# Stick-breaking attention in a fused decoder layer: loads spread over groups, and score products of 64 rows in two halves of the array

## The chip, the cores and the metric

The kernel runs on one core of a Trainium2 chip. The metric is the device time of one execution in microseconds (us), as the median of three runs.

## What is computed

One layer of a hybrid decoder, for one sequence of 2048 positions (and 16 learned ones ahead of them), width 1024, all in float32. An input projection makes the streams of two branches: a recurrent one (RWKV-7, 16 heads) and an attention one (16 heads of 64). The attention is of the stick-breaking kind, without a softmax:

```
scale = SB_HEAD_DIM ** -0.5
logits = einsum("bhqd,bhkd->bhqk", q[qs:qe], k[:qe]) * scale
log_keep = where(visible, log_sigmoid(-logits), 0)        # visible: key before query
log_between = cumsum(log_keep, reverse=True) - log_keep
weights = where(visible, exp(log_sigmoid(logits) + log_between), 0)
out = einsum("bhqk,bhkd->bhqd", weights, v[:qe])
```

Both branches are gated, projected, merged and projected again, normalised and added to the input.

## The kernel before

The kernel has four stages in order. Two calls of `project_phase` (half A, then half B of the positions) make the streams and leave them in DRAM. `attention_phase` does the attention of all heads. Then come the recurrence's chunk loop and the output products.

**Projections.** A product over 1024 is made of three fp32r products (high and low parts of both sides). For the attention's queries and keys, ScalarE writes the high part out of PSUM, and VectorE subtracts it from the PSUM value to get the low part (`query_lows`, L716; `key_lows`, L708). SyncE stores four tensors, `q_hi`, `q_lo`, `k_hi` and `k_lo` (L256 to L270). TensorE waits for both parts before it uses a PSUM bank again (L450).

**Attention.** A head has 16 tiles of 128 queries; four tiles are a *group* of a *rank* 0 to 3. Rank 0 sees few keys and rank 3 all of them. `rank` (L886) orders the eight groups of two heads as 0 1 2 3 3 2 1 0. The texts below call these eight groups T0 to T7; T0 to T3 belong to the even head and T4 to T7 to the odd one.

For each query tile the keys are cut into pieces of at most 512 (`pieces_of`, L872), from the last keys to the first. A piece passes through the engines in this way:
- TensorE makes the scores `z` (L1104, L1105). The 128 rows of `q_parts` hold the queries' high part (64 rows) and low part (64 rows); `k_high` and `k_low` hold the key's part twice, once for each half of the rows. Two fp32r products thus add up all four combinations.
- ScalarE takes the sigmoid of the negated scores into `keep` (L1172).
- VectorE runs a product scan along the keys, from the last key to the first, into `kept` (L1207 for a tile's first piece, L1210 for the others). A scan starts from the last column of the piece before.

For each tile of 128 keys of a group (`turn`, L1107), TensorE transposes `kept` of up to four query tiles into `turned` (L1115), ScalarE copies it to `w` (L1182), and TensorE multiplies by *value steps* (differences of neighbouring values) into `acc` (L1142). The value products come in pairs of key tiles, each product in its own half of the array's columns. Three key tiles of lag separate transposes and value products. On the diagonal another table of steps, `dv_diag`, is used, whose last row is another row of DRAM, `v_edge`. The group's sum is made on VectorE (L1216) and multiplied by a gate (L1220), which gives y.

There are two PSUM banks for `z`, four for `turned`, four buffers for `keep` and eight for `w`. Queries, keys and value steps have two buffers each, one for the even and one for the odd head.

The order on TensorE, ScalarE and VectorE is written out by `attention_schedule` (L907): the logits of the next group are dealt out between the key tiles of this one (`merged`, L893). All engines follow this order.

**SyncE's queue** does all loads and stores of the stage, in order (L1058 to L1073). After the y of each group it stores y and loads the gate of the group after next. The loads of a whole head (`load`, L1028) are nine DMAs and come in one piece: that of the odd head after T0, that of the next even head after T3. Within one, the value steps (L1046), the diagonal's 127 rows (L1047) and the edge row (L1048) come last. TensorE waits for a head's six query and key DMAs before the first logits (L1086), and for all its v DMAs before the first value product (L1093).

```python
sp.dma_start(dv[u][:, first + 1:last + 1, :], by_tile[:, tiles, :]).then_inc(v_sem, 16)
sp.dma_start(dv_diag[u][0:P - 1, tiles, :], by_tile[0:P - 1, tiles, :]).then_inc(v_sem, 16)
sp.dma_start(dv_diag[u][P - 1:P, tiles, :], edge[:, tiles, :]).then_inc(v_sem, 16)
```

Of the kernel before, what the change touches and what calls it, by code (L numbers as in the profile page):

```python
# [60 lines left out]
def project_phase(nc, sem, t, io, scratch, half):  # L61
# [14 lines left out]
    BY_PART = [i for i in range(NG) if OWNER[i] in (BQ, BKS)]  # L76
    NP = len(BY_PART)
# [5 lines left out]
    with ExitStack() as ctx:  # L83
# [16 lines left out]
        dv, q_lo = sb("dv", [P, N]), [sb(f"q_lo{g}", [P, 512], F32R) for g in range(len(RG))]  # L100
        k_hi, k_lo, v_raw = raw[1][:, 1:].bitcast(F32R), raw[2][:, 1:].bitcast(F32R), raw[0]
# [23 lines left out]
        bg_sent, kh_sent, kl_sent = s_("bg_sent"), s_("kh_sent"), s_("kl_sent")  # L125
        parted, dv_done, ql_sent, edge_sent = s_("parted"), s_("dv"), s_("ql_sent"), s_("edge_sent")
# [8 lines left out]
        square_high, square_low = q_lo  # L135
# [37 lines left out]
        def parted_by(eng, k, i):  # L173
            eng.wait_ge(parted, NP * k + BY_PART.index(i) + 1)

# [4 lines left out]
        def _(sp):  # L180
# [26 lines left out]
            sp.sem_inc(kh_sent, 16 * G)  # L207
            sp.sem_inc(kl_sent, 16 * G)
            sp.sem_inc(ql_sent, 16 * len(RG))
# [36 lines left out]
            with sp.Fori(0, PAIRS) as k:  # L246
                for j in range(BLOCKS):
# [7 lines left out]
                    if j == BKS:  # L255
                        store_staged(k, BQ, "q_hi", 0)  # L256
                        for g, (at, size) in enumerate(RG):
                            parted_by(sp, k, AT[BQ] + g)
                            sp.sem_inc(sp_go, 1)
                            c = T0 + at - CHUNK  # L260
                            sp.dma_start(scratch["q_lo"][rows(k), c:c + size], q_lo[g][:, 0:size].bitcast(F32)).then_inc(ql_sent, 16)
                    if j == BVS:
                        for g, (at, size) in enumerate(SG):
                            c = slice(T0 + at, T0 + at + size)
                            evacuated(sp, k, AT[BKS] + g)
                            sp.sem_inc(sp_go, 1)
                            sp.dma_start(scratch["k_hi"][rows(k), c], k_hi[:, at:at + size].bitcast(F32)).then_inc(kh_sent, 16)
                            parted_by(sp, k, AT[BKS] + g)
                            sp.sem_inc(sp_go, 1)
                            sp.dma_start(scratch["k_lo"][rows(k), c], k_lo[:, at:at + size].bitcast(F32)).then_inc(kl_sent, 16)  # L270
# [53 lines left out]
            sp.wait_ge(kh_sent, 16 * G * (PAIRS + 1))  # L324
            sp.wait_ge(kl_sent, 16 * G * (PAIRS + 1))
            sp.wait_ge(ql_sent, 16 * len(RG) * (PAIRS + 1))
# [7 lines left out]
        def _(pe):  # L334
# [107 lines left out]
            with pe.Fori(0, PAIRS) as k:  # L442
                for j in range(BLOCKS):
                    b = (j + 1) % 2
                    pe.wait_ge(low, BLOCKS * k + j + 2)
                    for g, (at, size) in enumerate(FIRST[j]):
# [3 lines left out]
                        if OWNER[before] in (BQ, BKS):  # L450
                            parted_by(pe, earlier, before)
                        elif OWNER[before] >= BQ:
# [21 lines left out]
        def _(act):  # L474
# [12 lines left out]
            def raw_copy(k, b, g, at, size):  # L487
# [6 lines left out]
                if g == 0 and b == BK:  # L494
                    sent_all(act, kh_sent, k, G)
                if g == 0 and b == BV:
                    sent_all(act, kl_sent, k, G)
# [18 lines left out]
            def squares(k, g, at, size):  # L516
# [3 lines left out]
                if g:  # L520
                    now(act, norm_pe, k, g - 1)
                else:
                    sent_all(act, ql_sent, k, len(RG))
# [7 lines left out]
            def to_stage(k, j, g, size, func):  # L531
# [5 lines left out]
                act.activation(dst.bitcast(F32R) if j == BQ else dst, bank[slot(i)][:, 0:size], func).then_inc(staged, 1)  # L537
# [57 lines left out]
            with act.Fori(0, PAIRS) as k:  # L595
# [15 lines left out]
                for g, (at, size) in enumerate(SG):  # L611
                    i = AT[BKS] + g
                    made(act, k, i)
                    act.copy(k_hi[:, at + lead(at):at + size], bank[slot(i)][:, lead(at):size]).then_inc(staged, 1)
# [25 lines left out]
        def _(dve):  # L640
# [75 lines left out]
            def query_lows(k, g, at, size):  # L716
                i = AT[BQ] + g
                evacuated(dve, k, i)
                now(dve, norm_pe, k, G - 1)
                sent_all(dve, ql_sent, k, len(RG))  # L720
                dve.tensor_tensor(q_lo[g][:, 0:size], bank[slot(i)][:, 0:size], stage[store_of(i)][:, 0:size],
                                  ALU.subtract).then_inc(parted, 1)

# [63 lines left out]
            with dve.Fori(0, PAIRS) as k:  # L787
                dve.tensor_copy(cols[:, :], t["par"][:, bass.ds(N_COLS * k, N_COLS)]).then_inc(cols_done, 1)
                dve.wait_ge(cols_done, k + 1)
                for j in range(BLOCKS):  # L790
# [5 lines left out]
                    for g, (at, size) in enumerate(SG):  # L796
# [10 lines left out]
                        if j == BQ and g < len(RG):  # L807
                            query_lows(k, g, *RG[g])
                        if j == BKS:
                            operands(k, g, at, size)  # L810
                            bonuses(k, g, at, size)
                            key_lows(k, g, at, size)
# [94 lines left out]
def attention_schedule():  # L907
# [46 lines left out]
def attention_phase(nc, sem, t, io, scratch):  # L954
# [7 lines left out]
    last_logits = {e[1]: e[5] for e in order if e[0] == "logits"}  # L962
    last_values = {e[1]: e[3] for e in order if e[0] == "values"}
    with ExitStack() as ctx:
        sb = lambda name, shape, dt=F32: ctx.enter_context(nc.sbuf_tensor(name, shape, dt))
        ps = lambda name, shape: ctx.enter_context(nc.psum_tensor(name, shape, F32))
        q_parts = [sb(f"q_parts{b}", [P, SEQ], F32R) for b in range(2)]
        k_high = [sb(f"k_high{b}", [P, META + SEQ], F32R) for b in range(2)]
# [1265 lines left out]
```

## Time and profile before

| | |
|---|---|
| median of three runs | 4381.3 us (4378.88 to 4382.68) |
| the profiled execution, its own time | 4379.16 us |
| its span, from first to last instruction | 4377.4 us |
| TensorE (PE) products busy | 4171.0 us, 95% |
| VectorE (DVE) busy | 2380.5 us, 54% |
| ScalarE (ACT) busy | 1666.2 us, 38% |
| GpSimd (POOL) busy | 804.4 us, 18% |
| mean granted clock of TensorE | 0.977 |

How to read it: busy time is the time in which an engine had an instruction running. Products on TensorE overlap, so that a product's own duration (0.39 us) is longer than the distance from one to the next (0.23 us); distances between starts tell its pace. PEld is the loading of weights, which runs beside the products. SPq is SyncE's queue: a DMA instruction's duration there is the time for which the queue was held by it, not the transfer's. "[0.24 <-x]" behind a row is the idle time of the engine ahead of it and what ended it. PEclk is the granted clock of TensorE as a share of full speed.

### The profile page before, as it was taken

What the parts mean: (1) busy time and instruction counts of PE and PEld (TensorE: products, weight loads), DVE (VectorE), ACT (ScalarE), POOL (GpSimd) and SP (SyncE); (2) the same over time, 40 slices, a digit from 0 to 9 for tenths busy, and PEclk for the clock granted to TensorE, in tenths of its full rate; (3) what the DMA queues carried; (4) which work ended last, traced back from release to release, by engine and by line L of the source; (5) the groups of instructions that cost most, each with busy time, mean ns of one, the idle gap of its engine ahead of it and who ended that gap; (6) DMA issues with size and microseconds to landing.
All of it is one profiled execution on the core that took longest, in us unless ns stands there. A gap on an engine that the chain in (4) does not pass through costs nothing. (4 is left out here: it accounts for less than half of the span.)

```text
span 4377.4 us, 90822 instructions
## 1 busy us (share of the span) xinstructions
PE 4171.0 (95%) x35784; PEld 3344.7 (76%) x35784; DVE 2380.5 (54%) x3103; ACT 1666.2 (38%) x3296; POOL 804.4 (18%) x637
## 2 busy tenths in 40 slices
PE   7999999997999999997999999999899999999999
PEld 7888888985888888885555555655688888878887
DVE  5444444443444444442777777777467766743222
ACT  4222222223222222222666666666444444421111
POOL 2110111111111111110000000000256666610222
PEclk9999999998999999998999999999899999999999
DMA  2333433333333333334443442442233333355653
GB/s 93 109 117 119 122 109 110 102 115 110 109 118 116 109 104 118 107 103 113 89 94 69 82 93 63 87 94 62 75 114 99 101 104 100 92 184 177 189 188 129
DMA packets 486971, 479.74 MB, mean 110 GB/s; under 512 B 260610, under 2 KB 370818, under 8 KB 480914
## 3 DMA queue, kind: packets, MB, share of 16 engines
q1 hardware_dynamic: 475154, 450.33, 37.1%
q10 hardware_dynamic: 11520, 25.17, 1.6%
q8 instruction: 221, 3.62, 0.3%
q14 instruction: 76, 0.62, 0.1%
HBM read 305.45 MB, written 169.93 MB: 109 GB/s over the span
## 5 line engine op out<-in xcount | busy, mean ns | idle before, releaser
L1210 DVE TENSOR_TENSOR_SCAN kept<-keep,kept 128x512 f32<-128x512 f32 (+1 forms) x448 | 436.6, 975 | 63.1 <-ACT keep L1172 22.6
L1172 ACT ACTIVATE keep<-z 128x512 f32<-128x512 f32 (+3 forms) x704 | 343.4, 506 | 302.4 <-PE z L1105 242.1
L1636 POOL TENSOR_TENSOR off<-NT,tri 128x512 f32<-128x512 f32 x165 | 206.1, 1276 | 1181.6 <-ACT NT L1540 1181.6
L1115 PE MATMUL turned<-t_identity,kept 128*128 128x128 f32 (+1 forms) x2432 | 383.0, 280 | 38.6 <-DVE kept L1210 38.6
L1115 PEld LDWEIGHTS turned<-t_identity,kept 128*128 128x128 f32 (+1 forms) x2432 | 280.7, 136 | 154.9 <-DVE kept L1210 50.0
L1182 ACT COPY w<-turned 128x512 f32<-128x512 f32 (+4 forms) x704 | 363.2, 528 | 92.4 <-PE turned L1115 90.7
L1207 DVE TENSOR_TENSOR_SCAN kept<-keep,hidden 128x512 f32<-128x512 f32 (+3 forms) x256 | 284.2, 1116 | 156.3 <-ACT keep L1172 155.7
L1104 PE MATMUL z<-k_high,q_parts 128*128 128x512 f32 (+3 forms) x704 | 308.6, 439 | 36.1 <-DMA k_low<-scr_k_lo 27.9
L1142 PE MATMUL acc<-w,dv 128*64 128x512 f32 (+3 forms) x1280 | 322.8, 562 | 15.4 <-issue 15.4
L1104 PEld LDWEIGHTS z<-k_high,q_parts 128*128 128x128 f32 x704 | 137.8, 196 | 191.5 <-ACT keep L1172 107.6
L1105 PE MATMUL z<-k_low,q_parts 128*128 128x512 f32 (+3 forms) x704 | 256.6, 368 | 0.0
L1471 PE MATMUL even<-T,off 64*64 64x64 f32 x5280 | 197.6, 222 | 14.7 <-DVE T L1603 3.6
L1550 ACT COPY T<-odd 128x256 f32<-128x256 f32 x264 | 98.2, 373 | 273.9 <-PE odd L1486 262.5
L1471 PEld LDWEIGHTS even<-T,off 64*64 64x64 f32 x5280 | 176.2, 135 | 32.8 <-issue 17.4
L1618 DVE STREAM_TRANSPOSE T<-T 128x256 f32<-128x256 f32 x264 | 117.4, 445 | 102.3 <-ACT T L1550 95.6
L1609 DVE TENSOR_TENSOR X<-even,eye 128x256 f32<-128x256 f32 x330 | 139.2, 422 | 42.1 <-PE even L1471 34.5
L1486 PE MATMUL odd<-X,T 64*64 64x64 f32 x4224 | 156.3, 223 | 3.0 <-issue 2.2
L1977 DVE TENSOR_TENSOR y_lo<-y_raw,y_hi 128x512 fp32r<-128x512 f32 x61 | 44.8, 734 | 209.8 <-ACT y_hi L1921 209.8
L1486 PEld LDWEIGHTS odd<-X,T 64*64 64x64 f32 x4224 | 137.1, 135 | 17.0 <-issue 3.1
L794 DVE CAST w_hi0B<-w_raw0B 128x1024 fp32r<-128x1024 f32 x40 | 41.7, 1043 | 193.4 <-PE pp3B L340 69.3
L1105 PEld LDWEIGHTS z<-k_low,q_parts 128*128 128x128 f32 x704 | 140.0, 199 | 4.7
L794 DVE CAST w_hi0A<-w_raw0A 128x1024 fp32r<-128x1024 f32 x40 | 32.5, 813 | 203.2 <-PE pp4A L340 76.4
(554 smaller groups left out, 10688.4 us busy)
## 6 DMA issues: line engine op xcount, KB each, us to landing
w_raw0A<-in_w_main SPq DMA_DIRECT2D x42, 512.0 KB, 3.9
w_raw0B<-in_w_main SPq DMA_DIRECT2D x42, 512.0 KB, 3.9
w_raw1A<-in_w_main SPq DMA_DIRECT2D x41, 512.0 KB, 4.0
w_raw1B<-in_w_main SPq DMA_DIRECT2D x41, 512.0 KB, 3.8
KB<-scr_kb SPq DMA_DIRECT2D x33, 512.0 KB, 5.2
AR<-scr_ar SPq DMA_DIRECT2D x33, 512.0 KB, 5.4
y_raw<-scr_y SPq DMA_DIRECT2D x64, 256.0 KB, 4.5
merge<-scr_merge SPq DMA_DIRECT2D x64, 256.0 KB, 6.3
```

The lines of the kernel that those rows point to most:

```text
L1104: pe.matmul(out, queries, k_high[u][:, k0:k0 + size], start=True, stop=False)
L1105: pe.matmul(out, queries, k_low[u][:, k0:k0 + size], start=False, stop=True).then_inc(logits_done, 1)
L1115: mm = pe.transpose(turned[num % TB][0:size, P * r:P * r + P], kept[kept_in(g)][:, src:src + size], t["identity"][:, :])
L1142: mm = pe.matmul(out, lhs, rhs, start=start, stop=stop, skip_group_check=True)
L1172: act.activation(keep[num % KB][:, 0:size], z[num % ZB][:, 0:size], ACT.Sigmoid, scale=-DH ** -0.5).then_inc(keep_done, 1)
L1182: act.copy(w[num % WB][0:size, c0:512], turned[num % TB][0:size, c0:512]).then_inc(copied, 1)
L1207: dve.tensor_tensor_scan(dst, data, hidden[:, 512 - size:][:, ::-1], 1.0, ALU.mult, ALU.max).then_inc(scanned, 1)
L1210: dve.tensor_tensor_scan(dst, data, data, kept[kept_in(g)][:, end:end + 1], ALU.mult, ALU.bypass).then_inc(scanned, 1)
L1471: mm = pe.matmul(x_bank(half)[hs, k, :], off[lv - 1][hs, HP * half + k, :], T2[hs, half, 0, k, :], start=True, stop=True)
L1486: mm = pe.matmul(p_bank(half)[hs, 0, k, :], T2[hs, half, 1, k, :], X[hs, half, k, :], start=True, stop=True)
L1609: dve.tensor_tensor(X[:, half, :, :], x_bank(half), eye[:, :].unsqueeze(1).broadcast_to([P, HP, C]), ALU.add).then_inc(s["x_out"], 1)
L1636: pool.tensor_tensor(out, a, b, op).then_inc(s[name], 1)
```

## The change

- Queries and keys are stored whole in fp32 (`q`, `k`), not in two parts each. `query_lows`, `key_lows`, their waits and half of the stores go.
- In the attention `queries` and `keys` hold a head's 64 rows twice, in the upper and the lower half of the partitions. A step of logits now takes a piece of each of two neighbouring query tiles: two plain fp32 products over 64 rows, one in either half of the array's rows, into the two banks of `z`. A step waits until both banks are free. Where the second tile has a piece more, the step has one product.
- The order deals out steps of two pieces; a scan waits for the previous piece of its own tile, not for the scan just before it.
- SyncE's loads of a head are spread: for the odd head queries after T7 of the pair before, keys after T0, steps after T1, the diagonal after T2; for the next even head queries and keys after T3, steps after T4, the diagonal after T5. For the first head the gates and a constant move. The edge row is loaded by GpSimd's queue, for each head as soon as its buffer is free, and has semaphores of its own.

```diff
-        square_high, square_low = q_lo
+        square_high, square_low = [sb(f"square{b}", [P, 512], F32R) for b in range(2)]
...
-            def key_lows(k, g, at, size):
-                i = AT[BKS] + g
-                evacuated(dve, k, i)
-                mixes(dve, k, BV, G - 1)
-                z = lead(at)
-                dve.tensor_tensor(k_lo[:, at + z:at + size], bank[slot(i)][:, z:size],
-                                  k_hi[:, at + z:at + size].bitcast(F32), ALU.subtract).then_inc(parted, 1)
...
-        for qt in range(GROUP * rank(g), GROUP * (rank(g) + 1)):
-            for k0, size in pieces_of(qt):
-                rows.append(("logits", g, qt, k0, size, nl))
-                nl += 1
+        for qt in range(GROUP * rank(g), GROUP * (rank(g) + 1), 2):
+            mine, next_tile = pieces_of(qt), pieces_of(qt + 1)
+            for i in range(len(next_tile)):
+                pieces = [(x, *some[i]) for x, some in ((qt, mine), (qt + 1, next_tile)) if i < len(some)]
+                rows.append(("logits", g, [(*piece, nl + j) for j, piece in enumerate(pieces)]))
+                nl += len(pieces)
...
+        def due_after(g):
+
+            pair, turn = divmod(g, 2 * GROUPS)
+            even, odd = 2 * pair + 2, 2 * pair + 1
+            if g == 0:
+                return [(odd, "queries"), (odd, "keys")]
+            plan = {0: [(odd, "keys")], 1: [(odd, "steps")], 2: [(odd, "diagonal")],
+                    3: [(even, "queries"), (even, "keys")], 4: [(even, "steps")], 5: [(even, "diagonal")],
+                    7: [(odd + 2, "queries")]}
+            return [(head, what) for head, what in plan.get(turn, []) if head < HEADS]
+
+        def free_after(head):
+
+            return GROUPS * (head - 1) if head % 2 == 0 else 2 * GROUPS * (head // 2) or 1
...
+            def load_diagonal(head, first, last, done):
+                u, rows, tiles = head % 2, slice(DH * head, DH * head + DH), slice(first, last)
+                by_tile = scratch["dv"][CHUNK:TOK, rows].rearrange("(k p) c -> p k c", p=P)
+                sp.dma_start(dv_diag[u][0:P - 1, tiles, :], by_tile[0:P - 1, tiles, :]).then_inc(done, 16)
...
-                if g % (2 * GROUPS) == 0:
-                    head = head_of(g) + 1
-                    load(head, 0, QT, qk_in[head % 2], v_in[head % 2])
-                if g % (2 * GROUPS) == GROUPS - 1 and head_of(g) + 2 < HEADS:
-                    head = head_of(g) + 2
-                    load(head, 0, QT, qk_in[head % 2], v_in[head % 2])
+                for head, what in due_after(g):
...
+                    pe.wait_ge(v_in[head % 2], 48 * loads_of(head))
+                    pe.wait_ge(edge_in[head % 2], 16 * loads_of(head))
...
-                reach(pe, keep_done, num - ZB + 1)
-                out = z[num % ZB][:, 0:size]
-                queries = q_parts[u][:, P * qt:P * qt + P]
-                pe.matmul(out, queries, k_high[u][:, k0:k0 + size], start=True, stop=False)
-                pe.matmul(out, queries, k_low[u][:, k0:k0 + size], start=False, stop=True).then_inc(logits_done, 1)
+                reach(pe, keep_done, pieces[-1][3] - ZB + 1)
+                for part, (qt, k0, size, num) in zip((slice(0, DH), slice(DH, P)), pieces):
+                    pe.matmul(z[num % ZB][:, 0:size], queries[u][part, P * qt:P * qt + P], keys[u][part, k0:k0 + size],
+                              start=True, stop=True).then_inc(logits_done, 1)
...
+                pool.dma_start(dv_diag[head % 2][P - 1:P, first:last, :], edge[:, first:last, :]).then_inc(done, 16)
+
+            for p, (first, last) in enumerate(FIRST_PARTS):
+                load_edges(0, first, last, edge_first[p])
+            for head in range(1, HEADS):
+                pool.wait_ge(y_done, free_after(head))
+                load_edges(head, 0, QT, edge_in[head % 2])
```

## Rows read from the trace of the kernel before

**Rows 1.** Busy time by stage: window, us, busy (count) by engine, PEclk, DMA share, GB/s.
```profile
1095.00:2022.00 927.00, 926.88 (x4127) 749.40 (x4125) 428.94 (x483) 241.82 (x387) 105.72 (x80) 1.00 0.38 112
...
2140.00:3101.00 961.00, 904.40 (x5209) 561.84 (x5207) 717.97 (x760) 624.47 (x1353) 0.00 (x0) 0.97 0.38 79
```
**Rows 2.** Timeline, VectorE, the y products: start, duration, instruction, idle before it.
```profile
2116.22 0.68 DVE L1220 TENSOR_TENSOR y_sb<-total,gate 64x512 f32<-64x512 f32 x1
...
2213.71 0.68 DVE L1220 TENSOR_TENSOR y_sb<-total,gate 64x512 f32<-64x512 f32 x1
...
2247.38 0.68 DVE L1220 TENSOR_TENSOR y_sb<-total,gate 64x512 f32<-64x512 f32 x1
...
2308.45 0.68 DVE L1220 TENSOR_TENSOR y_sb<-total,gate 64x512 f32<-64x512 f32 x1
...
2327.02 0.68 DVE L1220 TENSOR_TENSOR y_sb<-total,gate 64x512 f32<-64x512 f32 x1 [7.80 <-DMA gate<-scr_gates]
...
3030.58 0.68 DVE L1220 TENSOR_TENSOR y_sb<-total,gate 64x512 f32<-64x512 f32 x1
```
**Rows 3.** The waits of the attention: us in total, times, longest.
```profile
DVE y_sb L1220 <- DMA gate<-scr_gates: 61.2, 8, 8.3
```
**Rows 4.** Timeline, SyncE's queue, the load of a head after T0.
```profile
2214.42 0.46 SPq L1056 DMA_DIRECT2D scr_y<-y_sb  x1
...
2215.56 0.60 SPq L1035 DMA_DIRECT2D q_parts<-scr_q_hi  x1
...
2220.50 12.30 SPq L1047 DMA_DIRECT2D dv_diag<-scr_dv  x1
2232.84 33.95 SPq L1048 DMA_DIRECT2D dv_diag<-scr_v_edge  x1
...
2324.05 0.60 SPq L1052 DMA_DIRECT2D gate<-scr_gates  x1
```
**Rows 5.** Busy time by window during that load; the last two columns are DMA.
```profile
2225.00:2230.00 5.00, 5.00 (x30) 3.04 (x28) 4.76 (x7) 4.71 (x10) 0.00 (x0) 1.00 1.02 215
...
2250.00:2255.00 5.00, 5.00 (x30) 3.46 (x29) 4.69 (x5) 3.39 (x7) 0.00 (x0) 1.00 0.08 16
```
**Rows 6.** Timeline, TensorE, the first value products of T4 and of T0.
```profile
2269.49 1.08 PE L1142 MATMUL acc<-w,dv 128*64 128x512 f32 x4
...
2326.00 1.04 PE L1142 MATMUL acc<-w,dv 128*64 128x512 f32 x4 [2.04 <-issue]
```
**Rows 7.** Timeline, TensorE: transposes, a piece of logits, transposes, value products.
```profile
2517.99 0.60 PE L1115 MATMUL turned<-t_identity,kept 128*128 128x128 f32 x4
2518.34 0.48 PE L1104 MATMUL z<-k_high,q_parts 128*128 128x512 f32 x1
...
2518.89 0.60 PE L1115 MATMUL turned<-t_identity,kept 128*128 128x128 f32 x4
2519.42 1.08 PE L1142 MATMUL acc<-w,dv 128*64 128x512 f32 x4
```
**Rows 8.** Timeline, TensorE in the projections: two fp32 products over 64 rows.
```profile
1207.24 0.39 PE L340 MATMUL pp2B<-hn_hi,w_lo1B 128*128 128x512 f32 x1
1207.56 0.69 PE L352 MATMUL pa0B<-loraB,upB 64*128 64x512 f32 x1
1207.56 0.69 PE L353 MATMUL pa1B<-loraB,upB 64*128 64x512 f32 x1
1208.09 0.59 PE L352 MATMUL pa0B<-loraB,upB 64*128 64x512 f32 x1
...
1208.95 0.39 PE L339 MATMUL pp3B<-hn_lo,w_hi1B 128*128 128x512 f32 x1
```
**Rows 9.** The page's groups: the sigmoids.
```profile
L1172 ACT ACTIVATE keep<-z 128x512 f32<-128x512 f32 (+3 forms) x704 | 343.4, 506 | 302.4 <-PE z L1105 242.1
```
**Rows 10.** Busy time by window after the wait for the gate.
```profile
2334.00:2336.00 2.00, 2.00 (x9) 1.37 (x8) 1.90 (x3) 1.33 (x3) 0.00 (x0) 0.50 0.31 66
...
2338.00:2340.00 2.00, 2.00 (x13) 1.50 (x12) 1.56 (x2) 1.43 (x4) 0.00 (x0) 1.00 0.00 0
```

More of the change, by code:

```diff
@@ L255, in _ @@
                     if j == BKS:
[L256 to L261, printed above, removed]
+                        store_staged(k, BQ, "q", 0)
                     if j == BVS:
@@ L961, in attention_phase @@
     FIRST_PARTS = [(0, GROUP), (GROUP, 2 * GROUP), (2 * GROUP, QT)]
[L962 removed]
+    last_logits = {e[1]: e[2][-1][3] for e in order if e[0] == "logits"}
     last_values = {e[1]: e[3] for e in order if e[0] == "values"}
@@ L1017, in place @@
             return sum(keys_of(x) for x in range(GROUP * rank(g), qt))
+        scan_earlier, latest = {}, {}
+        for e in order:
+            if e[0] == "logits":
+                for qt, _, _, num in e[2]:
+                    scan_earlier[num] = latest.get((e[1], qt))
+                    latest[e[1], qt] = num
         def key_tile(kt):
@@ L1026, in _, with load_queries, load_keys @@
+        def free_after(head):
+            return GROUPS * (head - 1) if head % 2 == 0 else 2 * GROUPS * (head // 2) or 1
         @block.sync
         def _(sp):
-            def load(head, first, last, qk_sem, v_sem):
-                u = head % 2
-                rows = slice(DH * head, DH * head + DH)
-                low, high = slice(0, DH), slice(DH, P)
-                qs = slice(P * first, P * last)
+            def load_queries(head, first, last, done):
+                u, rows, qs = head % 2, slice(DH * head, DH * head + DH), slice(P * first, P * last)
+                for part in (slice(0, DH), slice(DH, P)):
+                    sp.dma_start(queries[u][part, qs], scratch["q"][rows, qs]).then_inc(done, 16)
+            def load_keys(head, first, last, done):
+                u, rows = head % 2, slice(DH * head, DH * head + DH)
@@ L1040, in load, with load_steps @@
-                tiles = slice(first, last)
+                for part in (slice(0, DH), slice(DH, P)):
+                    sp.dma_start(keys[u][part, ks], scratch["k"][rows, src]).then_inc(done, 16)
+            def load_steps(head, first, last, done):
+                u, rows, tiles = head % 2, slice(DH * head, DH * head + DH), slice(first, last)
                 by_tile = scratch["dv"][CHUNK:TOK, rows].rearrange("(k p) c -> p k c", p=P)
-                edge = scratch["v_edge"][:, rows].rearrange("(o k) c -> o k c", o=1)
@@ L1043, in load @@
                 if first == 0:
                     sp.wait_ge(cleared, 2)
[L1045 to L1048 removed]
+                    sp.dma_start(dv[u][0:META, 0, :], scratch["dv"][PAD:CHUNK, rows]).then_inc(done, 16)
@@ L1050, in load_gate @@
+                sp.dma_start(dv[u][:, first + 1:last + 1, :], by_tile[:, tiles, :]).then_inc(done, 16)
+            def load_diagonal(head, first, last, done):
+                u, rows, tiles = head % 2, slice(DH * head, DH * head + DH), slice(first, last)
+                by_tile = scratch["dv"][CHUNK:TOK, rows].rearrange("(k p) c -> p k c", p=P)
+                sp.dma_start(dv_diag[u][0:P - 1, tiles, :], by_tile[0:P - 1, tiles, :]).then_inc(done, 16)
             def load_gate(g):
```

152 lines of the change are left out of this document (67 added, 85 removed).

## The prediction

> **What bounds the kernel now.** I read the stages first [rows 1]. In the second half of the projections TensorE is busy 926.88 of 927 us, so what the change takes off VectorE and SyncE there buys nothing. The attention (2034 to 3101) is the stage in which the change works: TensorE is busy 904.40 of its last 961 us, VectorE 717.97. So TensorE's instruction stream is the rate there, except where it stands still for somebody.
>
> Next I read the period. Two heads are eight groups; I call them T0 to T7 (T0 to T3 the even head, T4 to T7 the odd one, ranks 0 1 2 3 3 2 1 0). The y product of T2 starts at 2116.22 in the first pair of heads and at 3030.58 in the eighth [rows 2]: 914.4 / 7 = 130.6 us for a pair of heads.
>
> Who stands still? The waits name one: VectorE waits 61.2 us in 8 waits for a gate's landing [rows 3]. In the pair shown it is the y of T6, at 2327.02, after 7.80 us of idling [rows 2]. SyncE's queue shows why [rows 4]: after the y of T0 (2213.71) it stores y at 2214.42 and starts the next head's load at 2215.56; the diagonal load (L1047) is held for 12.30 us and the edge load behind it (L1048) for 33.95 us; only then, at 2266.8, does the next y go out. For the other head the same hold lets the gate go at 2324.05 only.
>
> What holds it? While L1048 is held, the DMA engines are 0.08 busy and move 16 GB/s; before, with queries, keys and steps under way, it was 1.02 and 215 GB/s [rows 5]. 0.08 is about one engine of 16, and 16 GB/s times 33.95 us is 543 KB, about the 508 KB of the diagonal load (127 partitions x 16 tiles x 256 B). So the hold is the **diagonal transfer itself, 34 us on one DMA engine**, and the edge's instruction only waits behind it. The change leaves this transfer's shape as it is: 127 partitions.
>
> Here a rule of the Trainium skill bears on the change. "DMA: Bandwidth & Descriptors", section "Why a DMA increments its semaphore by 16 and not by 1", says that a DMA of the hardware queues uses the largest number of engines up to 16 that divides the slowest dimension, so that 127 partitions give one engine. The trace agrees (0.08 busy). By this rule the transfer stays at 34 us in the changed kernel wherever it is issued, which is the forecast; were the load spread over 16 engines the second rival below would hold.
>
> **The change part by part.** The sum is made against the profiled execution, 4379.16 us (span 4377.4), 2.1 under the median of 4381.3.
>
> *Projections:* two VectorE subtractions per block of queries and keys go, and so do half their stores. TensorE is never idle there [rows 1], so I take 0; the bound is 0 to -5, if the opening of a half has something to gain.
>
> *Diagonal of the odd head.* Before, it was issued after T0. Now it goes after T2's y: from a y's start to the third issue behind it are 2215.56 - 2213.71 = 1.85 us [rows 2, 4], then 34 us of transfer, about 0.6 to land: 36.5 us after the y's start. TensorE needs it for the first value product of T4 (it waits for all of the head's v loads at once). In the pair shown T2's y starts at 2247.38 [rows 2] and that product at 2269.49 [rows 6]: 22.1 us. Everything behind it in TensorE's order stands, logits and transposes too, so ScalarE and VectorE run dry. The path grows by 36.5 - 22.1 = **14.4 us** per pair of heads. What the logits cost in T3 lies inside this wait.
>
> *Diagonal of the even head.* Before after T3, now after T5's y, which starts at 2308.45; the first value product of the next T0 ran at 2326.00 [rows 2, 6], 17.55 us later, of which 2.04 were already a wait. Growth 36.5 - 17.55 = **18.9 us**; again the logits' cost in T6 and T7 is inside. The transfer could take 31 us (508 KB at 16 GB/s) or a few more than 34 with others beside it: -3 to +3 on each.
>
> *SyncE behind the diagonal.* The next store of y and gate load are held as L1048 was. After T2 that is T3's store and T5's gate, due 50 us later: covered. After T5 it is T6's store and the next T0's gate; that gate goes out as the diagonal ends and its product comes a whole group after that: covered. So the **gate wait goes: -7.8 us** per pair of heads [rows 2, 3] (0 if it comes back at T0). The edge loads now stand on GpSimd's queue, idle in this stage, and are issued a group or more ahead: 0. The trace shows no load on that queue; the nearest row is L1048 itself, which cost 2.04 us at TensorE [rows 6], so 0 to 2.
>
> *Logits.* Before, a piece of 512 keys is two products over 128 rows: from one set of transposes to the next with one piece between, 2517.99 to 2518.89, is 0.90 us, of which the four transposes take 0.35 to 0.43; a piece costs 0.47 to 0.55, two pieces 0.94 to 1.10 [rows 7]. The new form stands in the trace, in the projections [rows 8]: L352 and L353, fp32 over 64 rows each, start together (1207.56), each is two passes, 0.53 apart. From the full-array product before (1207.24) to the second one after (1208.95) are 1.71 us; without the pair it would be twice 0.23; the pair costs 1.25 us. So the halves do work side by side, but fp32 takes twice the passes at twice the length, and the column time is equal. What is added is the going in and out of the divided array. For value products the same shows: transposes to logits 0.35 us, transposes to value product 0.53 [rows 7]. Counting the order: 382 value blocks stay, and 704 logits steps between whole-array transposes become 384, of which 183 follow transposes (about +0.3) and 195 follow a value block, where part of the switch is paid already (+0.15); unequal pieces (144 with 272) cost the longer one's time (+2 us per pair of heads). Together 48 steps x about 0.25 = 12 us per pair of heads. Of these 48, 15 lie in T3, T6 and T7, inside the waits above; 33 remain: **+8.3 us**. The bounds are 0 (switches hidden by waiting) and 0.43 each, 14.
>
> The Trainium skill's "TensorEngine Tiling (Array Packing)", section "Key Properties", says that a change of tiling mode drains TensorE. Rows 7 and 8 agree (0.18 us at each entry). The same page's "Theoretical Speedup" gives up to 2x for a contraction of 64 rows; by that the pair would cost what one fp32 product does, which is the 1.06 us seen in rows 8, so nothing is left over against the two-pass form before.
>
> *Both score banks at once.* A pair waits until both banks are free, that is for two sigmoids of 0.506 us mean [rows 9]. 99 times only one transposes step or less stands between two pairs: pair ends, sigmoids 1.1, transposes cover 0.45, so about 0.7 us; per pair of heads 12 times, 8.7 us, half in places where VectorE's scans or the loads limit anyhow: **+3.5** (0 to 9).
>
> *Clock.* After the stall of before the granted clock is still 0.50 (the lower level, 1.2 GHz) from 2334 to 2336 and 1.00 from 2338 on [rows 10]. I take 4.5 us of work at half rate for each wait, so 2.3 us lost. Two waits of 11 and 18 us per pair: **+4.6** (2 to 9).
>
> *Scans:* the chains of two tiles alternate, so a scan no longer follows its own predecessor; VectorE has room: 0.
>
> Sum per pair of heads: 14.4 + 18.9 - 7.8 + 8.3 + 3.5 + 4.6 = +41.9. Seven periods: +293. In front of the first T2: queries and keys in four issues instead of six, the gates before the rest (the first gate wait, 5.7 of the 61.2, goes): -5. Behind the last T2: one odd diagonal and its clock, 14.4 + 2.3, and logits +10: +27. Together +315: 4379 + 315 = 4694, with the 2 us of the median **4696 us**.
>
> **The rivals.**
> *A, the forecast:* diagonals late and logits dearer. From bounds: transfer +-3 twice, logits -8 to +6, banks -3.5 to +5.5, clock -2.6 to +4.4, not all at once: 4600 to 4800.
> *B, the diagonals late, the logits free:* for it speaks that TensorE will wait anyhow, and that the two-pass form is a few per cent only; against it are rows 8. Without the 11.8 per period and 12 at the end: 4696 - 95 = 4601.
> *C, the hold was not the diagonal's* but the edge's, or the load moves faster when alone. Then the move to GpSimd's queue takes the hold away and no value product waits. It decides when the diagonal lands within 15.5 us of T5's y. With dearer logits (12 + 7 per pair, all of it now on the path, less 7.8, 2 and 3 of clock): +6 x 8 = 4430.
> *D, C with free logits:* gate waits -61, edge waits -15, clock and opening -10: 4295, faster by 2%. This is the one on the other side. Against C and D stand rows 5: a 4 KB edge cannot move 16 GB/s for 34 us.
> *E, the halves do not run side by side* in attention, so that the change does not do what it says: a pair costs 2.1 instead of 1.25 us, 33 steps x 0.85 = 28 per period: 4920. Against it are the equal starts in rows 8.
>
> **How the numbers follow.** A 0.66, B 0.17, C 0.08, D 0.05, E 0.04. The likeliest gives 4696. The range is 4570 to 4800: it holds nearly all of A and most of B, some 0.8. A measurement of this kernel can tell 0.2% (9 us) from no change. Faster 0.05 (D), same 0.02 (the lower edge of C), slower 0.93.
>
> **What would show it.** SyncE: the instruction behind each diagonal held about 34 us, DMA at 16 GB/s meanwhile. TensorE: 15 idle stretches, 8 of about 11 us ahead of T4 and 7 of about 18 ahead of T0, ended by a DMA into dv_diag; granted clock 0.5 after each. VectorE: no wait for a gate. Logits: both products of a pair starting together, 1.06 us, in 384 steps. Period of a pair of heads near 172 us. Wrong if the DMA share during the diagonal is well over 0.08, if dv_diag lands before the value products want it, or if logits to transposes shows no gap.

## The result

The changed kernel takes **4618.5 us** (median; 4614.83 to 4620.8), the kernel before beside it 4382.0 us. The ratio is 1.054 (95% interval 1.0522 to 1.0558), so the change costs 236 us. The profiled execution has a span of 4613.1 us.

The prediction was 4696 us, in a range of 4570 to 4800.

The y products give the period of a pair of heads, as [rows 2] did. Timeline of the changed kernel, VectorE: the first T2, then T2 and T5 of the pair that is shown below, the T2 of the pair after it, and the eighth T2.

```profile
2104.49 0.68 DVE L1220 TENSOR_TENSOR y_sb<-total,gate 64x512 f32<-64x512 f32 x1
...
2267.63 0.68 DVE L1220 TENSOR_TENSOR y_sb<-total,gate 64x512 f32<-64x512 f32 x1
...
2345.46 0.68 DVE L1220 TENSOR_TENSOR y_sb<-total,gate 64x512 f32<-64x512 f32 x1
...
2431.54 0.68 DVE L1220 TENSOR_TENSOR y_sb<-total,gate 64x512 f32<-64x512 f32 x1
...
3250.46 0.68 DVE L1220 TENSOR_TENSOR y_sb<-total,gate 64x512 f32<-64x512 f32 x1
```

(3250.46 - 2104.49) / 7 = 163.7 us, against 130.6 before: 33.1 us more per pair of heads, 232 us over seven of them. None of these products has an idle time before it: the wait for the gate [rows 3] is gone.

Where the time went is in the waits of the changed kernel during the attention (us in total, times, longest):

```profile
PE acc L1139 <- issue: 203.1, 15, 16.7
```

TensorE stands still 15 times ahead of a value product, 8 times ahead of T4 (11.0 to 12.0 us) and 7 times ahead of T0 (15.7 to 16.7 us). The profile names no releaser for these waits ("issue"); that they end with the diagonal is read from the times below. These are the first products of T4 and of T0, in the timeline of TensorE (the same places as [rows 6]):

```profile
2301.95 1.98 PE L1139 MATMUL acc<-w,dv 128*64 128x512 f32 x4 [11.98 <-issue]
...
2378.91 1.94 PE L1139 MATMUL acc<-w,dv 128*64 128x512 f32 x4 [15.99 <-issue]
```

SyncE's queue (as in [rows 4]) shows what came so late. L1043 stores y, L1039 loads a gate, L1035 is the diagonal:

```profile
2268.34 0.47 SPq L1043 DMA_DIRECT2D scr_y<-y_sb  x1
2268.86 0.60 SPq L1039 DMA_DIRECT2D gate<-scr_gates  x1
2269.50 0.45 SPq L1035 DMA_DIRECT2D dv_diag<-scr_dv  x1
2291.62 8.31 SPq L1043 DMA_DIRECT2D scr_y<-y_sb  x1
...
2347.32 0.44 SPq L1035 DMA_DIRECT2D dv_diag<-scr_dv  x1
2357.90 19.02 SPq L1043 DMA_DIRECT2D scr_y<-y_sb  x1
```

The diagonal is issued at 2269.50 (1.87 us after T2's y starts), and the next store is held until 2299.93 (2291.62 + 8.31), that is 30.4 us after the issue. The value product starts 2.0 us later. After T5 it is the same: issue at 2347.32, held until 2376.92, product at 2378.91. Busy time by window, columns as in [rows 5] (PEclk, DMA share and GB/s are the last three):

```profile
2275.00:2280.00 5.00, 5.00 (x28) 2.26 (x28) 4.47 (x4) 3.51 (x8) 0.00 (x0) 1.00 0.09 20
...
2295.00:2300.00 5.00, 0.00 (x0) 0.00 (x0) 0.00 (x0) 0.00 (x0) 0.00 (x0) 0.50 0.08 18
...
2303.00:2305.00 2.00, 2.00 (x10) 0.82 (x6) 0.00 (x0) 0.00 (x0) 0.00 (x0) 0.50 1.02 205
```

From 2295 to 2300 no engine computes, the DMA engines are 0.08 busy, and the granted clock is down to 0.50 (the lower level, 1.2 GHz). It is still there from 2303 to 2305, when TensorE works again.

The projections gave back a little: the last product of the second half starts at 2018.5 instead of 2021.5, and the first logits start at 2028.93 instead of 2034.10. The first T2 comes 11.7 us earlier than before [rows 2]; the first wait for a gate, 5.7 us, lay ahead of it too.

### The profile page after: what moved, and what is told of

The parts are those of the page before. It is cut to its first block and busy times, and to the rows that moved or that the text cites. A ratio compares the mean times of both kernels' runs of the same rounds, so it can differ in the third digit from the quotient of the medians.

```text
span 4613.1 us, 90322 instructions
## 1 busy us (share of the span) xinstructions
PE 4239.8 (92%) x35784; PEld 3220.8 (70%) x35784; DVE 2304.5 (50%) x3031; ACT 1674.8 (36%) x3296; POOL 824.8 (18%) x655
## 5 line engine op out<-in xcount | busy, mean ns | idle before, releaser
L1139 PE MATMUL acc<-w,dv 128*64 128x512 f32 (+3 forms) x1280 | 330.1, 574 | 203.1 <-issue 203.1
L1112 PEld LDWEIGHTS turned<-t_identity,kept 128*128 128x128 f32 (+1 forms) x2432 | 250.9, 137 | 355.8 <-ACT w L1179 203.9
L1169 ACT ACTIVATE keep<-z 128x512 f32<-128x512 f32 (+4 forms) x704 | 323.7, 505 | 379.6 <-PE z L1101 376.5
L1204 DVE TENSOR_TENSOR_SCAN kept<-keep,kept 128x512 f32<-128x512 f32 (+2 forms) x448 | 410.7, 959 | 44.6 <-ACT keep L1169 39.4
L1101 PE MATMUL z<-keys,queries 64*128 64x512 f32 (+4 forms) x1408 | 378.7, 579 | 54.7 <-ACT keep L1169 35.3
L1112 PE MATMUL turned<-t_identity,kept 128*128 128x128 f32 (+1 forms) x2432 | 393.4, 288 | 0.0
L1139 PEld LDWEIGHTS acc<-w,dv 128*64 128x64 f32 x1280 | 65.3, 138 | 257.1 <-issue 252.9
L1101 PEld LDWEIGHTS z<-keys,queries 64*128 64x128 f32 x1408 | 120.5, 193 | 171.3 <-ACT keep L1169 108.4
```

What stands on the lines that cost most here:

```text
L1101: pe.matmul(z[num % ZB][:, 0:size], queries[u][part, P * qt:P * qt + P], keys[u][part, k0:k0 + size], start=True, stop=True).then_inc(logi ...
L1112: mm = pe.transpose(turned[num % TB][0:size, P * r:P * r + P], kept[kept_in(g)][:, src:src + size], t["identity"][:, :])
L1139: mm = pe.matmul(out, lhs, rhs, start=start, stop=stop, skip_group_check=True)
L1169: act.activation(keep[num % KB][:, 0:size], z[num % ZB][:, 0:size], ACT.Sigmoid, scale=-DH ** -0.5).then_inc(keep_done, 1)
L1204: dve.tensor_tensor_scan(dst, data, data, kept[kept_in(g)][:, end:end + 1], ALU.mult, ALU.bypass).then_inc(scanned, 1)
```

## The experiments

There are two theories of the loss. Theory 1 is the prediction's: the diagonal, spread to a later place, comes late since it runs on one DMA engine. Theory 2 puts the loss on the new form of the logits. The ratio given with each experiment is to the kernel before beside it, which took 4375.7 to 4378.9 us; two experiments can be compared by their times to about 3 us.

### The diagonal back in its old place

```diff
-                return [(odd, "queries"), (odd, "keys")]
-            plan = {0: [(odd, "keys")], 1: [(odd, "steps")], 2: [(odd, "diagonal")],
-                    3: [(even, "queries"), (even, "keys")], 4: [(even, "steps")], 5: [(even, "diagonal")],
+                return [(odd, "queries"), (odd, "keys"), (odd, "diagonal")]
+            plan = {0: [(odd, "keys"), (odd, "diagonal")], 1: [(odd, "steps")],
+                    3: [(even, "queries"), (even, "keys"), (even, "diagonal")], 4: [(even, "steps")],
```

> The changed kernel, with the diagonal load alone put back to its old place (odd head after T0, even head after T3); everything else stays spread. Theory 1 (the late diagonal is the loss): the 203 us that TensorE stands ahead of the first value products of T4 and T0 go, and some 25 us of work at the lower clock behind them: about 4390 us, while one engine still takes 30 us per diagonal. Theory 2 (the new form of the logits is the loss, the waits only take up what would be lost otherwise): 4580 to 4620.

Measured: 4381.3 us, ratio to before 1.001 (1.0 to 1.002), 237 us less than the changed kernel. All 15 waits are gone. The y products of two T2 in a row give a period of 132.05 us, and all seven periods are the same:

```profile
2240.27 0.68 DVE L1220 TENSOR_TENSOR y_sb<-total,gate 64x512 f32<-64x512 f32 x1
...
2372.32 0.68 DVE L1220 TENSOR_TENSOR y_sb<-total,gate 64x512 f32<-64x512 f32 x1
```

The place of this one load makes the whole difference to the kernel before. The transfer still holds SyncE's queue (a store of y at 2218.25 is held 19.39 us), but no engine waits for it. Of the 31.7 us by which the period falls, 27.4 are the two waits themselves, on average over the seven periods (11.98 and 15.99 in the pair shown). The other 4.2 are what comes behind them: in the pair shown the granted clock is 0.50 until about 5 us after TensorE has started again, and ScalarE and VectorE start later still. How the 4.2 divide between the two was not measured.

### The diagonal late, but cut in two

```diff
-                sp.dma_start(dv_diag[u][0:P - 1, tiles, :], by_tile[0:P - 1, tiles, :]).then_inc(done, 16)
+                for a, z in ((0, 112), (112, P - 1)):
+                    sp.dma_start(dv_diag[u][a:z, tiles, :], by_tile[a:z, tiles, :]).then_inc(done, 16)
```

(and the counts of the two waits for the value loads.)

> The changed kernel, with the diagonal load at its new, late place but cut into one of 112 partitions and one of 15. Theory 1 with one DMA engine as the cause: each part is shared by many engines, SyncE's queue is no longer held for 30 us, the diagonal lands in some 5 us, and the time is about that of the early diagonal, 4390 us. If the transfer is slow for another reason (its 2032 small packets): no change, 4618 us. Theory 2: 4580 to 4620.

Measured: 4374.6 us, ratio 0.9995 (0.9986 to 1.0005). The load stays where the change put it, with the same bytes in the same small packets, and is harmless. SyncE's queue after T2 (L1036 is the diagonal, L1044 the next store of y):

```profile
2231.23 1.49 SPq L1036 DMA_DIRECT2D dv_diag<-scr_dv  x2
2253.35 0.47 SPq L1044 DMA_DIRECT2D scr_y<-y_sb  x1
```

No store is held, and in the five us behind the issue the DMA engines are 0.75 busy, where they were 0.08:

```profile
2231.00:2236.00 5.00, 5.00 (x27) 2.06 (x24) 4.38 (x5) 3.28 (x7) 0.00 (x0) 1.00 0.75 156
```

So it was the number of DMA engines, not the lateness alone and not the packets. This is what the Trainium skill's "DMA: Bandwidth & Descriptors" says in the section "Why a DMA increments its semaphore by 16 and not by 1": 127 partitions have no divisor up to 16 but one; 112 and 15 have 16 and 15. The trace agrees with one engine (0.08) and with many (0.75); it does not count them.

### The spread loads alone

The kernel before, with the change's functions for the loads and for the edges on GpSimd's queue; queries and keys keep their two parts, logits their old form.

> The kernel before with only the loads spread as in the change (edges on GpSimd's queue), queries and keys still in two parts and the logits in the old form. Theory 1: per pair of heads the gate wait goes (-6 us), the odd diagonal makes T4 wait (+12) and the even one T0 (+17), with 3 of clock: period 156 us instead of 131, about 4570 us. Theory 2: the spread only takes the gate waits away: 4320 us.

Measured: 4622.5 us, ratio 1.0564 (1.0546 to 1.0581). Theory 2 falls: without any new logits the loss is all there. It is 50 us larger than expected. The waits are longer than in the changed kernel:

```profile
PE acc L1173 <- issue: 282.7, 15, 22.5
```

SyncE's queue shows the reason, a diagonal that is held longer (issued at 2275.67, the store behind it free at 2309.36, that is 33.7 us):

```profile
2275.67 0.45 SPq L1068 DMA_DIRECT2D dv_diag<-scr_dv  x1
2297.87 11.49 SPq L1076 DMA_DIRECT2D scr_y<-y_sb  x1
```

It is 34 us as before and not 30 as in the changed kernel. That difference is taken up below.

### The new logits alone

The changed kernel with the old plan of loads: a whole head after T0 and after T3, the edge on SyncE's queue, and the gates behind the first head's loads.

> The changed kernel with the old plan of loads (a whole head in one piece after T0 and T3, the edge on SyncE's queue), so that only the queries and keys kept whole and the new form of the logits are left. Theory 1: some 8 us per pair of heads for going in and out of the divided array and for waiting on both banks, less 5 us in the projections; the gate waits stay: about 4440 us. Theory 2: near the changed kernel, 4580 to 4620. If the halves gave a gain of their own: under 4375.

Measured: 4380.4 us, ratio 1.0009 (0.9999 to 1.0018), where I had expected 4440. Its period is 132.05 us too. What I had missed is that the gate waits go here as well, but for one of 1.9 us. The load of a head has two DMAs less, and its diagonal is faster, so SyncE is held for 8.58 and 29.01 us instead of 12.30 and 33.95 [rows 4]:

```profile
2205.89 8.58 SPq L1031 DMA_DIRECT2D dv_diag<-scr_dv  x1
2214.51 29.01 SPq L1033 DMA_DIRECT2D dv_diag<-scr_v_edge  x1
```

The gate then lands before T6 wants it. The new logits alone therefore hide two things behind a zero: they take the stalls away and cost about as much. The next two kernels tell these apart.

### Old logits without any stall

The spread loads alone, as above, with the diagonal cut into 112 and 15.

> The kernel before with the spread loads and the diagonal cut into 112 and 15 partitions, logits in the old form. No gate wait (-61 us) and no wait of the first value products (-15 us) are left, so about 4305 us. The distance to the changed kernel with the same cut (4374.6) is then what the whole new treatment of queries, keys and logits costs, some 70 us, which was hidden there by those gains. If instead the new form is free: 4375.

Measured: **4303.7 us**, ratio 0.9834 (0.9818 to 0.9851). The period (T2 to T2) is 123.0 us on average over the seven, 122.4 us in the pair shown:

```profile
2218.76 0.68 DVE L1252 TENSOR_TENSOR y_sb<-total,gate 64x512 f32<-64x512 f32 x1
...
2341.20 0.68 DVE L1252 TENSOR_TENSOR y_sb<-total,gate 64x512 f32<-64x512 f32 x1
```

Against 4374.6 us with the new logits and the same loads, the new treatment of queries, keys and logits costs 71 us. Per pair of heads it is 132.05 - 122.99 = 9.1 us (9.6 in the pair shown), 63 us over the seven periods; the rest lies ahead of the first T2 and behind the last.

### Old products in the new order

The same, with steps of two pieces, the wait for both banks and the scans of two tiles alternating, but with the old products inside. Against the changed kernel, of which this is only the part on TensorE:

```diff
                 reach(pe, keep_done, pieces[-1][3] - ZB + 1)
-                for part, (qt, k0, size, num) in zip((slice(0, DH), slice(DH, P)), pieces):
-                    pe.matmul(z[num % ZB][:, 0:size], queries[u][part, P * qt:P * qt + P], keys[u][part, k0:k0 + size],
-                              start=True, stop=True).then_inc(logits_done, 1)
+                for qt, k0, size, num in pieces:
+                    out = z[num % ZB][:, 0:size]
+                    queries = q_parts[u][:, P * qt:P * qt + P]
+                    pe.matmul(out, queries, k_high[u][:, k0:k0 + size], start=True, stop=False)
+                    pe.matmul(out, queries, k_low[u][:, k0:k0 + size], start=False, stop=True).then_inc(logits_done, 1)
```

> The same kernel (spread, cut diagonal), with logits steps of two pieces, both banks waited for at once and the new order of the scans, but the products themselves in the old form (fp32r over 128 rows). Theory F (the divided array costs: going in and out, fp32 passes): nearly as without the new order, 4305 to 4325. Theory O (order and bank wait cost): 4360 to 4380, as the cut version of the changed kernel.

Measured: 4302.3 us, ratio 0.983 (0.9813 to 0.9846), period 122.5 us. With the old products the order, the bunching by two and the bank wait together cost nothing. So the 71 us come with the new products. The bank wait is smaller here, though: 16.6 us in 57 waits, where the new products have 38.1 in 66. The next kernel tests it there.

### Each product waits for its own bank

```diff
-                reach(pe, keep_done, pieces[-1][3] - ZB + 1)
                 for part, (qt, k0, size, num) in zip((slice(0, DH), slice(DH, P)), pieces):
+                    reach(pe, keep_done, num - ZB + 1)
```

> The changed kernel with the cut diagonal (4374.6 us), where each of the two products waits for its own bank instead of both for both. Theory O: the bank wait of some 0.7 us in 12 steps per pair of heads shrinks: 4320 to 4345. Theory F: no change within 10 us, since a product that starts alone makes the pair longer by what it waited less.

Measured: 4371.4 us, ratio 0.9988 (0.9979 to 0.9998); with the common wait it was 0.9995 (0.9986 to 1.0005), so no difference that these intervals can tell; the periods are 131.98 and 132.05 us. The common wait has this row in the cut version of the changed kernel (attention); here the same row is down to 1.4 us in 2 waits:

```profile
PE z L1102 <- ACT keep L1170: 38.1, 66, 1.2
```

37 us of a wait went and the time did not follow, as theory F said. Where it went shows in TensorE's busy time over the same stretch, first the cut version of the changed kernel, then this one:

```profile
2140.00:3000.00 860.00, 829.03 (x4588) 389.66 (x4588) 621.43 (x685) 559.35 (x1203) 6.30 (x13) 1.00 0.29 65
...
2140.00:3000.00 860.00, 853.86 (x4598) 406.72 (x4595) 618.78 (x681) 563.56 (x1202) 6.33 (x13) 1.00 0.29 65
```

TensorE is busy 24.8 us longer with nearly the same number of products: the first of a pair starts earlier, and the pair is done no sooner.

### Both products in the same half

```diff
-                for part, (qt, k0, size, num) in zip((slice(0, DH), slice(DH, P)), pieces):
+                for part, (qt, k0, size, num) in zip((slice(0, DH), slice(0, DH)), pieces):
```

> The changed kernel with the cut diagonal, with both products of a pair over the lower 64 rows, so that they cannot run side by side. If the halves work side by side in the changed kernel: 20 full pairs per head (of 512 or less) become longer by up to 0.85 us each, +200 to +270 us, about 4600 us. If they did not: 4375 us.

Measured: 4578.1 us, ratio 1.0464 (1.0446 to 1.0481), 203 us more. A full pair takes 1.92 us to the next transposes instead of 1.06. Timeline of TensorE:

```profile
2302.67 1.98 PE L1102 MATMUL z<-keys,queries 64*128 64x512 f32 x4
2304.59 0.66 PE L1113 MATMUL turned<-t_identity,kept 128*128 128x128 f32 x4
```

So the halves do run side by side in the changed kernel.

### Logits behind value blocks

The cut version of the changed kernel. TensorE holds a logits step back until it has issued the next value block, which also divides the array:

```diff
+            held, free = [], False
             for e in order:
                 if e[0] == "logits":
-                    logits(*e[1:])
+                    if held:
+                        logits(*held.pop(0)[1:])
+                        held.append(e)
+                        free = False
+                    elif free or e[1] == 0:
+                        logits(*e[1:])
+                        free = False
+                    else:
+                        held.append(e)
                 else:
+                    while e[2] < 0 and held:
+                        logits(*held.pop(0)[1:])
                     turn(*e[1:])
                     late.append(e[1:])
+                    count = len(late)
                     flush(LAG)
+                    free = len(late) < count
+                    if free and held:
+                        logits(*held.pop(0)[1:])
+                        free = False
```

> The changed kernel with the cut diagonal (4374.6 us), where TensorE alone issues a logits step behind the next value block instead of behind transposes. By the order of the program 183 steps between transposes become 41, 195 behind value blocks become 337, and changes between whole and divided array fall from 1325 to 1183. If going in and out of the divided array is what the new form costs: 142 changes less at 0.24 to 0.34 us, 35 to 48 us off, about 4333 us. If the cost is the column time of fp32: no change, or some us more because the logits come later.

Measured: 4347.5 us, ratio 0.9928 (0.9912 to 0.9945): 27 us less than without this order (29 by the ratios), and a period of 128.4 instead of 132.05 us. The expectation had 35 to 48 us off. The same products in this order are faster, so 27 of the 71 us hang on where the logits steps stand. The order has 142 changes of the array's form less, by the count of the expectation, which takes the step from a value block to a logits step as a change too (both divide the array, one in columns and one in rows); between whole and divided alone it has 284 less. That would be 0.19 or 0.10 us for each. But no price for one change follows. By the same count the new form has 562 changes more than the old one (1325 against 763), and at 0.19 us these would cost 107 us, more than the 71 measured. And the order moves waits as well: those for a bank of `z` fall from 38.1 to 21.9 us, and 10.4 us of waits for `w` are new.

### One line on the kernel before

```diff
-                sp.dma_start(dv_diag[u][0:P - 1, tiles, :], by_tile[0:P - 1, tiles, :]).then_inc(v_sem, 16)
+                for a, z in ((0, 112), (112, P - 1)):
+                    sp.dma_start(dv_diag[u][a:z, tiles, :], by_tile[a:z, tiles, :]).then_inc(v_sem, 16)
```

(and the counts of the two waits for the value loads.)

> The kernel before with nothing changed but the diagonal load cut into 112 and 15 partitions; loads in their old places. SyncE is then held for the 12 us of queries, keys and steps at most, not for 46, so the gate wait (61 us) and the 2 us waits at T0 (15 us) go: 4303 us, the same as with the spread loads. If the spread itself were worth something: 4303 plus that.

Measured: **4301.3 us**, ratio 0.9823 (0.9807 to 0.984), within the intervals the same as with spread loads (0.9834, 0.983). The queue is held for 14.74 us, while queries, keys and steps drain (the DMA engines are about 1.0 busy), and no longer for 46:

```profile
2246.47 14.74 SPq L1048 DMA_DIRECT2D dv_diag<-scr_dv  x2
2261.26 1.35 SPq L1049 DMA_DIRECT2D dv_diag<-scr_v_edge  x1
```

Once the diagonal is cut, spreading the loads is worth nothing here.

### Why 30 us here and 34 there

Two kernels looked for it, each the changed kernel with something unused added.

```diff
             "k": dram("k", (D, TOK)),
+            "spare_q": dram("spare_q", (D, SEQ)),
+            "spare_k": dram("spare_k", (D, TOK)),
```

> The changed kernel with two unused tensors in DRAM, of the size of the two that the change drops, so that everything behind them lies where it lay before. The diagonal took 30 us in the changed kernel and 34 us before; if the place in DRAM makes this: 34 us again, 15 waits longer by 3.5 each, about 4670 us. Otherwise 4618 us.

Measured: 4615.5 us, ratio 1.0539 (1.0518 to 1.056). No change; a diagonal here takes 29.5 us.

```diff
         keys = [sb(f"keys{b}", [P, META + SEQ]) for b in range(2)]
+        spare = [sb(f"spare{b}", [P, META + SEQ]) for b in range(2)]
```

> The changed kernel with two unused tiles on chip, of the size of the second key tiles that the change drops, so that the value tables lie where they lay before. If their place makes the diagonal take 34 instead of 30 us: about 4670 us. Otherwise 4618 us.

Measured: 4690.4 us, ratio 1.071 (1.0689 to 1.0732): two tiles that nothing touches cost 72 us, 20 more than expected. SyncE's queue: the diagonal (L1036) is issued at 2285.22 and the store behind it is free at 2319.14, 33.9 us later:

```profile
2285.22 0.45 SPq L1036 DMA_DIRECT2D dv_diag<-scr_dv  x1
2307.32 11.82 SPq L1044 DMA_DIRECT2D scr_y<-y_sb  x1
```

The waits ahead of the value products are 275.2 us here, 203.1 without the spare tiles. The spare tiles move all tiles behind them, the value tables among them, and leave the source in DRAM where it is. So the layout on chip changes how fast the one engine gets through the diagonal; that it is the place of the target, `dv_diag`, is likely but was not tested by itself. The change moved it, by dropping two key tiles, and got 3.5 to 5 us per transfer for it (after T5 of the same pair it is 34.7 us here and 29.6 there). This also fits the sum: with the 34 us diagonal, the changed kernel (4690.4) is 68 us above the spread loads alone (4622.5), or 64 by the ratios, close to the 71 us of the logits. Without the spare tiles these are paid for by the faster diagonal, and the two kernels seem equal.

## Why the prediction was right, and where its sizes were off

**The mechanism** of the loss held: the 34 us hold was the diagonal's, one engine moves it at 16 to 20 GB/s wherever it is issued, and 15 waits of TensorE came of it, 8 ahead of T4 and 7 ahead of T0. Putting this load back (4381.3) or sharing it between engines (4374.6) removes the whole loss.

**The diagonal's term** was 14.4 + 18.9 = 33.3 us per pair of heads and measured 28.1: from T2's y to T4's first value product are 2301.95 - 2267.63 = 34.3 us (22.1 before), from T5's y to T0's 2378.91 - 2345.46 = 33.5 us (17.55 before). I had put 36.5 for both. The transfer takes 30.4 and 29.6 us instead of 34, for a reason that no row of before could show; the value product comes 2.0 us behind the end of the hold, where 0.6 was put for the landing.

**The gate wait** went, as forecast, and did not come back at T0: SyncE's store after T5 is held 19.02 us, and no y product waits. Stall-free, the old logits have a period of 123.0 us, so all stalls of before cost 7.6 us per pair of heads, the 2 us ahead of T0 among them. The prediction took 7.8 for the gate alone and had the T0 wait inside the diagonal's term, so its gain from the gate was some 2 us too large.

**The logits** were forecast at 12 us per pair of heads for form and unequal pieces, and measured 9.1. The rows of TensorE's timeline in the changed kernel, to be read beside [rows 7], have the same steps:

```profile
2307.98 0.66 PE L1112 MATMUL turned<-t_identity,kept 128*128 128x128 f32 x4
2308.57 1.13 PE L1101 MATMUL z<-keys,queries 64*128 64x512 f32 x4
2309.63 0.66 PE L1112 MATMUL turned<-t_identity,kept 128*128 128x128 f32 x4
2310.22 1.08 PE L1139 MATMUL acc<-w,dv 128*64 128x512 f32 x4
```

Transposes to logits are 0.59 us where they were 0.35, the pair takes 1.06 us as L352 and L353 did [rows 8], and transposes to value products 0.59 where they were 0.53. The 0.3 us for a step between transposes was right (0.24 + 0.06). These are single steps of one place. That the cost hangs on how the steps lie between transposes and value blocks, the other order shows (27 us). How the 9.1 us divide between the changes of form, the longer of two unequal pieces and the rest was not measured. The 8.3 us that the prediction put outside the waits assumes that 3.7 hide in them; this was not measured by itself.

**The bank wait** is the term that was wrong in kind: +3.5 us forecast, nothing measured. The wait exists (35 us in 66 waits in the changed kernel), but the old products with such a wait take no longer, and taking it away from the new ones gains 0.07 us per pair of heads. What failed is the step that took a wait for the second bank as lost time: without it the first product starts earlier and the pair ends when it did.

**The clock** and the refilling: the two waits end with the clock at 0.50, and the cost beyond the waits is 4.2 us per pair, 4.6 forecast for the clock alone.

Together: 33.1 us per pair of heads against 41.9. The experiments add up to it: +31.7 for the late diagonal (132.05 to 163.7), +9.1 for the logits (123.0 to 132.05), -7.6 for the stalls of before (130.6 to 123.0). Of the gap of 8.8, 5.2 are the diagonal's term and 3.5 the bank wait; the errors of logits, clock and gate nearly cancel. Over seven periods the gap is 62 us. The other 16 lie at the ends: the first T2 came 11.7 us earlier than before where 5 was forecast, and behind the last T2 the kernel is 16 us longer where 27 was.

With the spare tiles, where the diagonal takes the 34 us that the prediction assumed, the period is 173.1 us and the time 4690.4, against some 172 and 4696 forecast. That this is so close is partly luck: the landing, 1.4 us too short on each of two transfers, stands against the bank wait that cost nothing.

**The rivals.** B (logits free) gave 4601, closer to the measured 4618.5 than the forecast, for a wrong reason: the logits do cost 64 to 71 us. C and D needed a hold that was not the diagonal's, or a diagonal that landed in time, as a load over 16 engines would have. E needed products that run one after the other; both in the same half (4578.1) show what E would have cost, 203 us.

**The range's cases** left out one thing that later mattered: that a change of tile sizes moves other tiles. It was worth as much (72 us) as the whole new form of the logits.

## What to carry to other kernels

Look at the DMA share while a queue is held: a share near one sixteenth (0.08 here) points to a load on one engine, and its first dimension is the place to look. Here such a load, issued early, held the queue and cost 78 us through late gates; spreading the loads without mending it turned the queue's hold into the array's wait and cost 236 us more, while cutting 127 rows into 112 and 15 took the 78 us off the kernel before with nothing else changed. When two parts of a change give the same total as one of them alone, time each part with the stalls removed before calling it free.

## What was not expected of the hardware

- A transfer of 2032 packets of 256 B by one DMA engine took 29.6 to 30.4 us in the changed kernel and 33.9 to 34.7 us in the one with spare tiles, which moves its target by 2 x 8256 B per partition (33.4 to 34.0 with the old key tiles); more tensors in DRAM changed nothing (29.5 us). Why the layout matters stays open; only two were tried.
- TensorE's waits for a PSUM bank, 38 us in total, could be removed without a gain; its busy time grew instead.
